# A two-block transformer kernel on one core: its weight stream fetched two units (1024 KB) at a time

## The chip, the core and the metric

The kernel runs on one core of a Trainium2 chip (trn2). The metric is the time of one execution on the device, in microseconds; of several runs the median counts. TensorE does the matrix products, VectorE, ScalarE and GpSimd the rest, and SyncE issues the transfers between HBM and SBUF, the memory on the core. In the profile the engines are called PE (PEld is its loading of weights), DVE, ACT, POOL and SP.

## The reference

A block on 256 rows of 2048 features, and a second block behind it. All is float32. Cut to what matters:

```python
def first_block(x, ...):
    h = rmsnorm(x, norm_mix_pre)
    proj = h @ w_in                                   # 2048 x 5120
    mix = concatenate([pool_mixer(...), hgrn2_mixer(...)]) @ w_out    # 2048 x 2048
    x = x + rmsnorm(mix, norm_mix_post)
    h = rmsnorm(x, norm_mlp_pre)
    ff = square(relu(h @ w_mlp_in)) @ w_mlp_out       # 2048 x 8192 x 2048
    return x + rmsnorm(ff, norm_mlp_post)

def second_block(x, c, ...):
    m = silu(c) @ ada_w + ada_b                       # six vectors of 2048: shifts, scales, gates
    n = modulate(rmsnorm(x), m[0], m[1])
    u, v = split(gelu(n @ a_w_in))                    # 2048 x 8192
    x = x + m[2] * ((u * spatial(rmsnorm(v))) @ a_w_out)
    n = modulate(rmsnorm(x), m[3], m[4])
    g, w = split(dwconv(n @ ffn_w_up))                # 2048 x 11264
    x = x + m[5] * ((silu(g) * w) @ ffn_w_down)       # 5632 x 2048
    return rmsnorm(x, final_g)
```

## The kernel before

**The weight stream.** All weights of the seven large products are cut on the host into 824 units (`wstream`, one unit is 128 partitions x 1024 float32, that is 256 rows of a weight matrix by 512 of its columns, 512 KB, 4 KB in a row per partition). The units are numbered in the order in which they are used. Eight units (six in the last four groups) make a group, a whole sum over 2048 inputs into 512 output columns, held in two PSUM banks (four in the up projection of the last stage). The groups: 0 to 9 input projection, 10 to 13 output projection of the mixers, 14 to 45 the MLP, 46 to 53 and 54 to 69 the gated stage, 70 to 103 the convolutional feed-forward.

**What happens to a unit.** Products are made in three passes at reduced format: each operand is a high part plus a low part. Unit n goes through slot n % 4 (`RING = 4`) of three rings in SBUF:

- SyncE (`unit(n)`, L290 to L294) waits until the low part of unit n-4 is made (the last reader of the slot in `raw`), and issues the transfer into `raw`.
- ScalarE (`split(n)`, L667 to L674) waits for the transfer and until TensorE has used unit n-4, and copies `raw` to the high part `whi`.
- VectorE (`split(n)`, L1064 to L1070) subtracts: `wlo = raw - whi`, and raises `lo_ready`.
- TensorE (`token_unit` L389, `feature_unit` L360, `wide_unit` L375) waits for `lo_ready` and multiplies; the last matmul of a unit raises `unit_used`.

Each engine runs its instructions in the order written. `body` (L676 and L1083) writes the splits of ScalarE and VectorE four units ahead of TensorE: while TensorE is at unit i of group j, they split unit i + 4. In between stand the work on the sums, the transposes' copies, and the norms.

**The other transfers.** SyncE issues everything from one list (L311 to L356). In groups 14 to 61 it also loads 192 pieces of `ada_w` (512 KB each, `ada(k)`, L296 to L300) into a ring of two, `aring`; VectorE adds each to `aacc` (L1080) behind the split that stands four units ahead. `ada_tile` (L62) puts them at units 1, 3, 5 and 7 of a group, in each eighth group at 0, 1, 2 and 3. Single rows of 2048 elements spread over 128 partitions (1024 KB, `row`, L302), `gvb` (L308, 256 KB) and pieces of `ws` (L305, 128 KB) stand at fixed units. A wait of SyncE holds back all that stands behind it.

**The start.** ScalarE squares the four parts of `x` as they come, splits unit 0 (L793), and only then takes the root of the norm (L794); VectorE, after that root, makes the normalised `xn`, which TensorE transposes first (L431).

**The places named below.** Before group 10 the heads are gated (`gate_heads`, L1260), squared, summed and scaled (`norm_heads`, L1274) and transposed (`heads_to_features`, L521), with splits of units 83 to 85 between these steps; L836 is the sigmoid of the gate's sums. In group 14 the root of the norm and the two functions of `relu2` (L873) stand between the splits of units 122 and 123. At the end of the MLP TensorE transposes `aacc` (`ada_columns`, L459) after the last piece was added. In group 46 `gelu_v` (L925) stands between the splits of units 378 and 379.

Of the kernel before, what the change touches and what calls it, by code (L numbers as in the profile page):

```python
# [19 lines left out]
RING = 4  # L20
# [41 lines left out]
def ada_tile(j, i):  # L62

    if not G_MLP <= j < G_MLP + VECS * 8:
        return None
    at = (0, 1, 2, 3) if (j - G_MLP) % 8 == 7 else (1, 3, 5, 7)
    return (j - G_MLP) * ADA_PER_GROUP + at.index(i) if i in at else None


def build(nc, xt, wstream, astream, cT, adab, gains, rows, gvrow, cwp, bsp, wsT, poolw, poolp, lbl, masks, corr,  # L70
          eye_in, out):
    ctx = ExitStack()
    with ctx:
# [4 lines left out]
        def region(size):  # L78
            o = at[0]
            at[0] += size  # L80
            assert at[0] <= base + SPAN, at[0] - base
            return o

        def place(name, offset, shape, dt=F32):
            return nc.alloc_sbuf_tensor_at(name, shape, dt, offset=offset)

        sem = lambda n: ctx.enter_context(nc.semaphore(n))
        KB = 1024

        raw = place("raw", region(16 * KB), [P, RING, UW])  # L90
# [91 lines left out]
        bank = [ctx.enter_context(nc.psum_tensor(f"bank{i}", [P, NC], F32)) for i in range(4)]  # L182
        mis = [ctx.enter_context(nc.psum_tensor(f"mis{i}", [P, NC], F32)) for i in range(4)]

        raw_arrived = [sem(f"raw_arrived{i}") for i in range(RING)]
        ada_arrived = [sem(f"ada_arrived{i}") for i in range(2)]
        x_arrived = [sem(f"x_arrived{i}") for i in range(4)]
        par_arrived = sem("par_arrived")
# [6 lines left out]
        lo_ready = sem("lo_ready")  # L195
# [92 lines left out]
        @block.sync  # L288
        def _(sp):
            def unit(n):  # L290
                if n >= RING:
                    sp.wait_ge(lo_ready, n - RING + 1)
                sp.dma_start(raw[:, n % RING, :], wstream[n:n + 1, :, :].rearrange("o p w -> p (o w)")
                             ).then_inc(raw_arrived[n % RING], 16)  # L294

            def ada(k):  # L296
                if k >= 2:
                    sp.wait_ge(ada_used, k - 1)
                sp.dma_start(aring[:, k % 2, :], astream[k:k + 1, :, :].rearrange("o p w -> p (o w)")
                             ).then_inc(ada_arrived[k % 2], 16)  # L300

            def row(r, dst):  # L302
                sp.dma_start(dst[:, :], rows[r:r + 1, :].to_broadcast([P, D])).then_inc(row_arrived[r], 16)

            def spatial_part(g):  # L305
                sp.dma_start(ws[:, 2 * g:2 * g + 2, :], wsT[:, 2 * g:2 * g + 2, :]).then_inc(ws_arrived, 16)

            def gv_part(g):  # L308
                sp.dma_start(gvb[:, :], gvrow[0:1, g * NC:(g + 1) * NC].to_broadcast([P, NC])).then_inc(gv_arrived, 16)

            for i in range(4):  # L311
                b, h = i % 2, i // 2
                sp.dma_start(x[:, b, h * 1024:(h + 1) * 1024], xt[:, b, h * 1024:(h + 1) * 1024]
                             ).then_inc(x_arrived[i], 16)
            for dst, src in ((gain, gains), (cf, cT), (eye, eye_in), (cw, cwp), (ab, adab), (bs, bsp)):
                sp.dma_start(dst[:], src).then_inc(par_arrived, 16)
            for n in range(RING):
                unit(n)
            for dst, src in ((pw, poolw), (pp, poolp), (lb2, lbl), (mk, masks), (cor, corr)):
                sp.dma_start(dst[:], src).then_inc(mix_arrived, 16)  # L320
            for n in range(RING, UNITS):
                unit(n)
                m = n - RING
                j, i = (m // GU, m % GU) if m < G_DT * GU else (G_DT, GU)
                if n == 78:
                    sp.wait_ge(h_sc, 18)
                    sp.wait_ge(p_d, 1)
                    row(ROW_MIX, gmix)
                if n == G_MLP * GU + RING:
                    sp.wait_ge(mix_lo, 8)  # L330
                    row(ROW_MLP, gmlp)
                    ada(0)
                    ada(1)
                if (k := ada_tile(j, i)) is not None and k >= 2:
                    ada(k)
                if n == (G_AV + 2) * GU:
                    sp.wait_ge(xs_lo, 24)
                    row(ROW_GATE, gate2)
                    gv_part(0)
                if G_AV < j <= G_AV + 4 and i % 4 == 2:  # L340
                    spatial_part(2 * (j - G_AV - 1) + i // 4)
                g = 4 * ((j - G_AU) // 8) + (j - G_AU) % 8
                if G_AU <= j < G_FF and (j - G_AU) % 8 < 4 and i == 3 and g < 7:
                    sp.wait_ge(vs_ready, g + 1)
                    gv_part(g + 1)
                if j == G_AU + 4 and i == 3:
                    row(ROW_GATE2, gate5)
                if j == G_AU + 12 and i == 3:
                    row(ROW_END, gend)
            sp.wait_ge(out_act, 1)  # L350
            sp.dma_start(out[:, 0, 0:3 * NC], acc[:, 0, 0:3 * NC]).then_inc(out_sent, 16)
            sp.wait_ge(out_dve, 1)
            sp.dma_start(out[:, :, 3 * NC:], acc[:, :, 3 * NC:]).then_inc(out_sent, 16)
            sp.wait_ge(out_dve, 2)
            sp.dma_start(out[:, 1, 0:3 * NC], acc[:, 1, 0:3 * NC]).then_inc(out_sent, 16)
            sp.wait_ge(out_sent, 48)  # L356
# [291 lines left out]
        def _(act):  # L648
# [18 lines left out]
            def split(n):  # L667
                if n >= UNITS:
                    return
                slot = n % RING  # L670
                act.wait_ge(raw_arrived[slot], 16 * (n // RING + 1))
                if n >= RING:
                    act.wait_ge(unit_used, n - RING + 1)
                act.activation(whi[:, slot, :], raw[:, slot, :], ACT.Copy).then_inc(hi_ready, 1)  # L674

            def body(j, evac, after=None, done=0, last=True):  # L676
                units = units_of(j)
                for i in range(units):
                    if i == units - 1 and evac:
                        evac()  # L680
                    if i >= done and (last or i < units - 1):
                        split(first_unit(j) + RING + i)
                    if after:
                        after(i)
# [28 lines left out]
            def features(z, j, first=None):  # L713

                feature_tmp(z, 0)
                for i in range(8):
                    if 0 < i < 7:
                        feature_tmp(z, i + 1)
                    act.wait_ge(tm_ready, 8 * z + i + 1)
                    act.activation(xs[:, 2 * i:2 * i + 2, 0:T], tiles(t1[:, i % 2, :]), ACT.Copy).then_inc(xs_hi, 1)  # L720
                    if i == 0:
                        feature_tmp(z, 1)
                    if first:
                        first(i)
                    if 2 <= i < 2 + RING:
                        split(first_unit(j) + RING + i - 2)
# [60 lines left out]
            for i in range(4):  # L787
# [3 lines left out]
                           ssq[:, S_X, b, h:h + 1])  # L791
            sums_read(S_X)
            split(0)  # L793
            root(S_X)  # L794
            split(1)
# [880 lines left out]
```

## Time and profile before

| | |
|---|---|
| median of 3 runs | 2459.76 us (2459.64 to 2462.09) |
| the profiled execution, its own time | 2461.96 us |
| its span in the profile | 2460.2 us |
| busy: TensorE, VectorE, ScalarE, GpSimd | 2396.0, 1663.1, 1191.2, 58.8 us |
| HBM read | 544.89 MB, 222 GB/s over the span |
| mean granted clock of TensorE | 0.990 |

The span goes from the first to the last instruction; the execution's own time is 1.8 us more. Busy times of different engines overlap. A row of a group of instructions (section 5 of the page) ends with the idle time of the engine just before them and what ended most of it; a time in square brackets in a timeline is the same for one instruction. The landing of a transfer is the time from its issue by SyncE to the last of its 16 completion signals. Times are counted from the first instruction.

### The profile page before, as it was taken

The numbers are of one execution on the slowest core, as the hardware profiler recorded it, in microseconds if no ns is written. First come the engines' busy times: TensorE is split into PE (matmuls) and PEld (weight loads), VectorE is DVE, ScalarE is ACT, GpSimd is POOL, SyncE is SP. The second block draws the span as 40 slices with busy tenths as digits, with TensorE's granted clock in tenths as the row PEclk, the third lists the DMA queues.
The fourth block names the chain that finished last, engine by engine and source line by source line (L and its number), as shares of the span: only waits on it lengthen the run. The fifth ranks groups of instructions, "written<-read, shape, count | busy, mean of one in ns | idle before, by whom it ended". The sixth has DMA issues, their size and how long they took to land.

```text
span 2460.2 us, 30688 instructions
## 1 busy us (share of the span) xinstructions
PE 2396.0 (97%) x12000; PEld 2032.0 (83%) x12000; DVE 1663.1 (68%) x1960; ACT 1191.2 (48%) x1508; POOL 58.8 (2%) x42
## 2 busy tenths in 40 slices
PE   7999999999999999997999999999999999999997
PEld 7989787888888888886888888887888888888886
DVE  5884666777677677677667776555767567765675
ACT  6553455544444534545554443445655355544553
POOL 0330000000000000000000000000000000000000
PEclk9999999999999999999999999999999999999999
DMA  6434555887887887875987886564555655565553
GB/s 226 137 129 163 170 188 179 307 286 273 284 288 272 277 294 279 272 273 189 351 291 264 276 297 223 186 198 153 188 188 188 195 184 188 187 194 191 184 177 137
DMA packets 152189, 549.00 MB, mean 223 GB/s; under 512 B 17776, under 2 KB 19056, under 8 KB 151280
## 3 DMA queue, kind: packets, MB, share of 16 engines
q1 hardware_dynamic: 152048, 547.05, 65.8%
q8 instruction: 97, 1.59, 0.3%
q14 instruction: 44, 0.36, 0.0%
HBM read 544.89 MB, written 2.10 MB: 222 GB/s over the span
## 4 chain that ended last, share of the span: by engine, by line
PE 93%; DVE 3%; ACT 2%; issue 1%; DMA 0%; SPq 0%; POOL 0%; DVEq 0%; ACTq 0%
PE bank L398 20%; PE bank L400 19%; PE bank L399 19%; PE bank L383 7%; PE mis L383 7%; PE bank L385 3%; PE mis L385 3%; PE bank L370 2%; PE bank L371 2%; PE bank L372 2%; PE mis L400 2%; PE mis L399 2%; PE mis L398 2%; PE mis L484 1%; PE mis L454 1%
## 5 line engine op out<-in xcount | busy, mean ns | idle before, releaser
L1069 DVE TENSOR_TENSOR wlo<-raw,whi 128x1024 fp32r<-128x1024 f32 x824 | 1005.2, 1225 | 688.4 <-ACT whi L674 685.9
L674 ACT ACTIVATE whi<-raw 128x1024 fp32r<-128x1024 f32 x824 | 868.1, 1059 | 1060.0 <-PE bank L400 660.4
L398 PE MATMUL bank<-whi,xs 128*128 128x512 f32 x1152 | 456.5, 396 | 4.3 <-DVE wlo L1069 2.8
L400 PE MATMUL bank<-wlo,xs 128*128 128x512 f32 x1152 | 450.1, 391 | 0.0
L399 PE MATMUL bank<-whi,xs 128*128 128x512 f32 x1152 | 450.0, 391 | 0.0
L398 PE MATMUL bank<-whi,hs 128*128 128x512 f32 x1072 | 419.5, 391 | 2.1 <-DVE hs L1549 2.1
L399 PE MATMUL bank<-whi,hs 128*128 128x512 f32 x1072 | 418.0, 390 | 0.0
L400 PE MATMUL bank<-wlo,hs 128*128 128x512 f32 x1072 | 417.9, 390 | 0.0
L398 PEld LDWEIGHTS bank<-whi,xs 128*128 128x128 f32 x1152 | 217.4, 189 | 50.1 <-issue 6.5
L400 PEld LDWEIGHTS bank<-wlo,xs 128*128 128x128 f32 x1152 | 217.1, 188 | 45.8
L399 PEld LDWEIGHTS bank<-whi,xs 128*128 128x128 f32 x1152 | 217.5, 189 | 44.0 <-issue 0.2
L383 PE MATMUL bank<-xs,whi 128*128 128x512 f32 x704 | 251.7, 402 | 0.8 <-issue 0.8
L383 PE MATMUL mis<-xs,whi 128*128 128x512 f32 x704 | 249.2, 399 | 0.0
L1080 DVE SCALAR_TENSOR_TENSOR aacc<-aring,sc_c,aacc 128x1024 f32<-128x1024 f32 x192 | 245.6, 1279 | 1.3 <-DMA aring<-astream 1.0
L398 PEld LDWEIGHTS bank<-whi,hs 128*128 128x128 f32 x1072 | 201.6, 188 | 44.1 <-DVE hs L1549 2.5
L400 PEld LDWEIGHTS bank<-wlo,hs 128*128 128x128 f32 x1072 | 201.7, 188 | 42.0
L399 PEld LDWEIGHTS bank<-whi,hs 128*128 128x128 f32 x1072 | 201.7, 188 | 41.8 <-issue 0.2
L385 PE MATMUL bank<-xs,wlo 128*128 128x256 f32 x704 | 198.7, 282 | 0.0
L385 PE MATMUL mis<-xs,wlo 128*128 128x256 f32 x704 | 197.9, 281 | 0.0
L383 PEld LDWEIGHTS bank<-xs,whi 128*128 128x128 f32 x704 | 133.3, 189 | 34.0 <-issue 1.2
L383 PEld LDWEIGHTS mis<-xs,whi 128*128 128x128 f32 x704 | 132.3, 188 | 32.8
L385 PEld LDWEIGHTS bank<-xs,wlo 128*128 128x128 f32 x704 | 134.1, 191 | 0.1
(180 smaller groups left out, 2118.6 us busy)
## 6 DMA issues: line engine op xcount, KB each, us to landing
raw<-wstream SPq DMA_DIRECT2D x824, 512.0 KB, 4.3
aring<-astream SPq DMA_DIRECT2D x192, 512.0 KB, 4.9
x<-xt SPq DMA_DIRECT2D x4, 512.0 KB, 6.4
gate<-rows SPq DMA_DIRECT2D x2, 1024.0 KB, 7.7
gvb<-gvrow SPq DMA_DIRECT2D x8, 256.0 KB, 5.2
out<-acc SPq DMA_DIRECT2D x2, 768.0 KB, 4.4
pw<-poolw SPq DMA_DIRECT2D x1, 1024.0 KB, 9.6
gmix<-rows SPq DMA_DIRECT2D x1, 1024.0 KB, 7.8
```

The lines of the kernel that those rows point to most:

```text
L370: pe.matmul(o, whi[:, slot, c], h, start=st, stop=False, skip_group_check=True)
L371: pe.matmul(o, whi[:, slot, c], l, start=False, stop=False, skip_group_check=True)
L372: mm = pe.matmul(o, wlo[:, slot, c], h, start=False, stop=sp_, skip_group_check=True)
L383: pe.matmul(banks[m][:, :], whi[:, slot, c], xs[:, kt0 + k, :], start=st, stop=False, skip_group_check=True)
L385: mm = pe.matmul(banks[m][:, 0:T], wlo[:, slot, c], xs[:, kt0 + k, 0:T], start=False, stop=sp_, skip_group_check=True)
L398: pe.matmul(o, h, whi[:, slot, c], start=first and k == 0, stop=False)
L399: pe.matmul(o, l, whi[:, slot, c], start=False, stop=False)
L400: mm = pe.matmul(o, h, wlo[:, slot, c], start=False, stop=last and k == UK - 1)
L454: mm = pe.transpose(mis[pair + m // 2][:, (m % 2) * T + b * P:(m % 2) * T + (b + 1) * P], t1[:, b, m * P:(m + 1) * P], eye[:, :])
L674: act.activation(whi[:, slot, :], raw[:, slot, :], ACT.Copy).then_inc(hi_ready, 1)
L1069: dve.tensor_tensor(wlo[:, slot, :], raw[:, slot, :], whi[:, slot, :].bitcast(F32), ALU.subtract).then_inc(lo_ready, 1)
L1080: dve.scalar_tensor_tensor(out=a, in0=aring[:, k % 2, :], scalar=sc_c[:, kt:kt + 1], in1=a, op0=ALU.mult, op1=ALU.add).then_inc(ada_used, 1)
```

## The change

The weights come in transfers of two units. `unit(n)` does nothing for an odd n; for an even n it issues one transfer for units n and n + 1 into slots n % 4 and n % 4 + 1. It waits until the low part of unit n-3 is made, since both slots must be free, and both units have one semaphore: ScalarE's split of either waits for the whole transfer. Source and destination have 128 partitions with two runs of 4 KB each.

```diff
-        raw_arrived = [sem(f"raw_arrived{i}") for i in range(RING)]
+        raw_arrived = [sem(f"raw_arrived{i}") for i in range(RING // 2)]
...
             def unit(n):
+
+                if n % 2:
+                    return
                 if n >= RING:
-                    sp.wait_ge(lo_ready, n - RING + 1)
-                sp.dma_start(raw[:, n % RING, :], wstream[n:n + 1, :, :].rearrange("o p w -> p (o w)")
-                             ).then_inc(raw_arrived[n % RING], 16)
+                    sp.wait_ge(lo_ready, n - RING + 2)
+                sp.dma_start(raw[:, n % RING:n % RING + 2, :], wstream[n:n + 2, :, :].rearrange("o p w -> p o w")
+                             ).then_inc(raw_arrived[n % RING // 2], 16)
...
                 slot = n % RING
-                act.wait_ge(raw_arrived[slot], 16 * (n // RING + 1))
+                act.wait_ge(raw_arrived[slot // 2], 16 * (n // RING + 1))
```

Lines behind the edit move down by three. The order of SyncE shows what stands where. At the start, before and with the change (`x` is the input, the small ones are parameters, `pw` and what follows belongs to the mixers):

```order
L313 DMA x<-xt 128x1024 x4
L316 DMA gain<-gains 128x64
...
L316 DMA ab<-adab 128x64
L316 DMA bs<-bsp 128x16
L293 DMA raw<-wstream 128x1024 x4
L320 DMA pw<-poolw 128x2048
```

```order
L316 DMA x<-xt 128x1024 x4
L319 DMA gain<-gains 128x64
...
L319 DMA ab<-adab 128x64
L319 DMA bs<-bsp 128x16
L296 DMA raw<-wstream 128x2x1024 x2
L323 DMA pw<-poolw 128x2048
```

Units 0 and 1 are one transfer now. In groups 46 to 48, units 382 to 388 of the stream, before:

```order
L293 DMA raw<-wstream 128x1024 x2
L299 DMA aring<-astream 128x1024
L293 DMA raw<-wstream 128x1024
L306 DMA ws<-wsT 128x256
L293 DMA raw<-wstream 128x1024
L299 DMA aring<-astream 128x1024
L293 DMA raw<-wstream 128x1024
L303 DMA gate_63<-rows 128x2048
L309 DMA gvb<-gvrow 128x512
L293 DMA raw<-wstream 128x1024
L299 DMA aring<-astream 128x1024
L293 DMA raw<-wstream 128x1024
```

The single `raw` ahead of `ws` is unit 382, the one behind it 383, the one ahead of `gate_63` 384, the one behind `gvb` 385, the last 386. With the change:

```order
L296 DMA raw<-wstream 128x2x1024
L302 DMA aring<-astream 128x1024
L296 DMA raw<-wstream 128x2x1024
L309 DMA ws<-wsT 128x256
L302 DMA aring<-astream 128x1024
L296 DMA raw<-wstream 128x2x1024
L306 DMA gate_63<-rows 128x2048
L312 DMA gvb<-gvrow 128x512
L302 DMA aring<-astream 128x1024
L296 DMA raw<-wstream 128x2x1024
```

The pair ahead of `ws` is 382 and 383, the one ahead of `gate_63` 384 and 385, the last 386 and 387. Each odd unit has moved up to the even one: unit 383 stands ahead of the piece of `ws`, unit 385 ahead of the row for `gate2` and of `gvb`. The pieces of `ada_w` stand behind the pair whose second unit they followed. On the other engines the order of instructions is the same.

## Rows read from the trace of the kernel before

**Rows 1.** The page: span, engines, and the costliest groups of the two splits.

```profile
span 2460.2 us, 30688 instructions
...
PE 2396.0 (97%) x12000; PEld 2032.0 (83%) x12000; DVE 1663.1 (68%) x1960; ACT 1191.2 (48%) x1508; POOL 58.8 (2%) x42
...
L1069 DVE TENSOR_TENSOR wlo<-raw,whi 128x1024 fp32r<-128x1024 f32 x824 | 1005.2, 1225 | 688.4 <-ACT whi L674 685.9
L674 ACT ACTIVATE whi<-raw 128x1024 fp32r<-128x1024 f32 x824 | 868.1, 1059 | 1060.0 <-PE bank L400 660.4
```

**Rows 2.** List of waits, whole span: who for whom, us in all, times, longest.

```profile
ACT whi L674 <- DMA raw<-wstream: 72.1, 39, 4.9
...
PE bank L398 <- DVE wlo L1069: 2.8, 3, 1.7
...
PE bank L398 <- DVE hs L1549: 2.1, 1, 2.1
```

**Rows 3.** Tile view of raw: time from issue to landing over 824 transfers.

```profile
DMA to landing us min/median/max: 3.0/4.3/9.9
```

**Rows 4.** Timeline of the start (first and last row); tile view, transfer issued at 6.85.

```profile
12.08 1.06 ACT L674 ACTIVATE whi<-raw 128x1024 fp32r<-128x1024 f32 x1 [1.01 <-DMA raw<-wstream]
...
DMA to landing us min/median/max: 6.5/6.5/6.5
...
15.26 1.09 PE L431 MATMUL mis<-eye,xn 128*128 128x128 f32 x4 [15.26 <-DVE xn L1125]
```

**Rows 5.** Timeline around unit 82: SyncE, VectorE, ScalarE, TensorE.

```profile
297.40 0.33 SPq L293 DMA_DIRECT2D raw<-wstream  x1
...
298.73 4.62 DVE L1069 TENSOR_TENSOR wlo<-raw,whi 128x1024 fp32r<-128x1024 f32 x4
...
300.76 1.06 ACT L674 ACTIVATE whi<-raw 128x1024 fp32r<-128x1024 f32 x1 [1.61 <-DMA raw<-wstream]
304.22 1.28 ACT L836 ACT_TABLE_LOAD   x1 [2.40 <-PE bank L400]
...
318.95 0.33 PE L526 MATMUL mis<-eye,oo 128*128 128x128 f32 x1 [1.22 <-DVE oo L1274]
```

**Rows 6.** Timeline around unit 122: ScalarE, VectorE, TensorE.

```profile
428.30 1.06 ACT L674 ACTIVATE whi<-raw 128x1024 fp32r<-128x1024 f32 x1 [0.24 <-DMA raw<-wstream]
...
434.08 1.23 DVE L1069 TENSOR_TENSOR wlo<-raw,whi 128x1024 fp32r<-128x1024 f32 x1 [3.39 <-ACT whi L674]
...
436.72 0.48 PE L398 MATMUL bank<-whi,xs 128*128 128x512 f32 x1
```

**Rows 7.** Timeline of TensorE at the end of the MLP.

```profile
1117.50 1.75 PE L461 MATMUL mis<-eye,aacc 128*128 128x128 f32 x14 [0.86 <-DVE aacc L1080]
```

**Rows 8.** Timeline around unit 378 by engine; DMA view (KB, us to landing) from 1161.3.

```profile
1160.84 0.91 SPq L293 DMA_DIRECT2D raw<-wstream  x2
...
raw<-wstream SPq DMA_DIRECT2D x1, 512.0 KB, 5.6
...
1164.97 1.06 ACT L674 ACTIVATE whi<-raw 128x1024 fp32r<-128x1024 f32 x1 [4.63 <-DMA raw<-wstream]
...
1170.92 1.23 DVE L1069 TENSOR_TENSOR wlo<-raw,whi 128x1024 fp32r<-128x1024 f32 x1 [3.63 <-ACT whi L674]
...
1172.55 0.39 PE L398 MATMUL bank<-whi,xs 128*128 128x512 f32 x1
```

**Rows 9.** Timeline around unit 387: SyncE, ScalarE, VectorE, TensorE.

```profile
1179.10 0.33 SPq L293 DMA_DIRECT2D raw<-wstream  x1
...
1187.37 1.06 ACT L674 ACTIVATE whi<-raw 128x1024 fp32r<-128x1024 f32 x1 [1.51 <-DMA raw<-wstream]
...
1191.89 1.23 DVE L1069 TENSOR_TENSOR wlo<-raw,whi 128x1024 fp32r<-128x1024 f32 x1 [2.21 <-ACT whi L674]
...
1194.31 0.39 PE L398 MATMUL bank<-whi,xs 128*128 128x512 f32 x1
```

**Rows 10.** Windows view: us, busy by engine, PEclk, DMA share, GB/s.

```profile
2392.00:2396.00 4.00, 4.00 (x12) 3.13 (x11) 0.64 (x2) 0.60 (x1) 0.00 (x0) 0.57 0.66 218
```

## The prediction

> **What bounds the kernel now.** I read the page first. TensorE is busy 2396.0 of 2460.2 us [rows 1], so the kernel is matmul bound, and a change of the weight transfers can only act through the 64 us in which TensorE stands still. The next question is how far the weight stream is from making it stand. The rows of the two split instructions say: ScalarE (L674, 1059 ns) waits mostly for a free slot, that is for TensorE (660.4 us), VectorE (L1069, 1225 ns) waits for ScalarE [rows 1]. In the list of waits ScalarE waits for a weight transfer 39 times, 72.1 us in all, but TensorE waits for VectorE's low part only 3 times, 2.8 us in all [rows 2]. So late weights are common and almost always hidden. Hidden by what, and by how much, decides the case.
>
> **The two covers in the steady state.** A unit of 12 matmuls takes TensorE 2.72 us: unit 379 starts at 1172.55 and unit 387 at 1194.31, eight units in 21.76 us [rows 8, 9]. ScalarE starts to split unit n when TensorE ends unit n-4; call that time t. The low part is done at t + 1.06 + 1.23 = t + 2.3, TensorE wants it at t + 3 x 2.72 = t + 8.2: the second cover is 5.9 us. The transfer of unit n leaves when the low part of unit n-4 is done, at t + 2.3 - 10.9 = t - 8.6, and lands 4.3 us later in the median [rows 3]: the first cover is 8.6 - 4.3 = 4.3 us.
> With the change the pair (n, n+1) leaves when the low part of unit n-3 is done, at t - 5.9, since its second slot must be free too. It carries 1024 KB. What that costs: at the start the transfers run back to back, and units 0 and 1 land at 12.06 and 6.85 + 6.5 = 13.34 [rows 4], so 512 KB more are 1.28 us more. The pair should land after 4.3 + 1.3 = 5.6 us, 0.3 us before it is wanted. No row shows a 1024 KB weight transfer; its bounds are the shortest landing, 3.0, plus 1.3 = 4.3 us and twice the median, 8.6 us. I take 5.6, since both pieces are rows of 4 KB as before and the extra bytes have a measured price. The loop of one pair of slots (landing 5.6, two splits 2.1, the last low part 1.2) is 8.9 us, and TensorE needs 10.9 us for its four units. So the steady stretches, nearly all of the kernel, gain and lose nothing: the first cover is spent, the second still stands. The Trainium skill, "DMA: Bandwidth & Descriptors", section "Measured", gives 6.15 us of data movement for 1 MB; the trace moves 512 KB in 1.28 us at the start, so it does not agree, and by the page's figure alone the pair would land over 3 us later than I take, past its first cover and still inside the second.
>
> **Where a cover is missing.** I went through all places where TensorE starts less than 3 us after the low part, or waits. Six of them hang on a transfer. Each is priced in the time frame of before.
> 1. **Start.** TensorE's first work waits for VectorE, at 15.26. Behind it stands a chain: ScalarE splits unit 0 at 12.08, when its transfer lands, and only then takes the root for the norm [rows 4]. The pair lands with unit 1, at 13.34: **+1.3**.
> 2. **Heads before the output projection.** Unit 82 left at 297.40 and ScalarE waited for it until 300.76. VectorE ends the low part of unit 79 at 298.73 + 1.2 = 299.9; the pair (82, 83) leaves then and lands after at least 3.3 + 1.3 us, at 304.6, that is 3.8 later. ScalarE stood idle 2.40 us before 304.22, which absorbs 2.4; the other 1.4 us go down the chain of gates and norms to the transposes at 318.95, for which TensorE already waits 1.22 us [rows 5]: **+1.4**.
> 3. **First MLP group.** ScalarE waits for unit 122 until 428.30; its pair lands 1.3 us later by the price of the bytes, or up to twice that if unit 123 queues as it does now, and the chain after the split (root, two relus, split of 123) follows without a gap that would absorb it. The low part of unit 123 is done at 434.08 + 1.23 = 435.31 and wanted at 436.72 [rows 6], cover 1.4: between 0 and +1.1, I take **+0.6**.
> 4. **End of the MLP.** TensorE waits 0.86 us for the last modulation step of VectorE [rows 7], which stands in its order behind the low parts of units 366 and 367. Unit 366 lands up to 1.3 later as the first half of a pair; what VectorE idles between them takes some of it: between 0 and 1.3, **+0.7**.
> 5. **First gated group.** Unit 378 lands at 1164.95, unit 379, issued at 1161.3, after 5.6 us, at 1166.9: the pair is 2.0 later. ScalarE works without a gap from there to the split of 379; its low part ends at 1170.92 + 1.23 = 1172.15, wanted at 1172.55 [rows 8]. Cover 0.4: **+1.6**.
> 6. **The burst behind it.** Here a 1024 KB row, a 256 KB row and modulation weights share the queue. Unit 387 left at 1179.10 and needed the longest landing of all, 9.9 us [rows 3, 9]; unit 386 was split at 1187.37. The pair lands not before 1189.0, +1.6, and up to 2 us later still, because the pair (382, 383) is late by about 2 and the low part of 383 releases this pair. Cover at unit 387: 1194.31 - 1191.89 - 1.23 = 1.2. Between +0.4 and +2.4, I take **+1.6**.
> Sum: 1.3 + 1.4 + 0.6 + 0.7 + 1.6 + 1.6 = **+7.2 us**. Against the gains: SyncE issues 412 transfers less, but it waits for slots nearly all the time, so that is worth nothing. Unit 385 now stands ahead of the 1024 KB row instead of behind it, but TensorE did not wait for it, so this gains nothing either.
> The modulation transfers keep their places behind the odd units; they are asked for four splits ahead of their use, and where two follow each other (last group of eight) SyncE waits for the ring of two anyway.
>
> The profiled execution took 2461.96 us (span 2460.2); its forecast is 2469.2. The median of the three runs is 2459.76, 2.2 us less, and from there the sum gives **2467.0 us**, slower by 0.3%. About 0.2%, 4.9 us, is what can be told from no change.
>
> **Rivals.**
> A. *Not slower: the landing hardly grows.* Some 1.7 us of each landing do not depend on the bytes (3.0 shortest, less 1.28 for the data), and they are paid once per pair. If the crowded landings (4.3 and above, up to 9.9) contain such waits, a pair lands with or before its old second unit. Then places 3, 4 and 6 cost nothing and 5 under 1, while 1 and part of 2 stay, since they come from bytes and from the later issue: +2 to +4, about 2463. For it: the shortest and the median landing differ by 1.3 us at the same size. Against it: three of the six prices are simply "the pair is there when its second half was there". Chance 0.29. It decides if pairs land within about 4.5 us in quiet stretches.
> B. *The ring becomes the bound in the crowded stretches.* From group 14 to 61 the modulation weights share the queue. If pairs land there after 8.0 us and more, the loop is 8.0 + 2.1 + 1.2 = 11.3 against 10.9 us, 0.4 us for each four of 384 units, 38 us if it holds everywhere, 13 us if in a third of them, on top of the 7. Against it: a queue that works through the same bytes does not land the second half later than now. Result 2480 (at worst 2505). Chance 0.12. The Trainium skill, "Perfetto Trace Analysis", section "DMA Optimizations", says that splitting transfers may let work start sooner; the change does the opposite, and places 1 and 2 are where the trace agrees, with units 0 and 82 awaited as they land (12.06, 300.74).
> C. *The clock.* After TensorE's idle gap of 2.1 us (the wait for the product's low part) it ran at a mean of 0.57 of its clock for 4 us, so mostly at 1.2 instead of 2.4 GHz [rows 2, 10]. 4 x 0.43 = 1.7 us is the price. Place 2 makes the gap before 318.95 1.2 + 1.4 = 2.6 us, so the clock may fall there: +1.7, 2468.7. This is inside the forecast's range.
> D. *Faster.* The only waits for weights that could go are 2.8 and 0.86 us, and the start costs 1.3: at best -2.4 us, which is no change. Beyond 0.2% only if a stretch at half clock vanishes as well. Chance 0.04.
> That the change does not do what it says is excluded by the order of SyncE: 412 issues of two units, no other engine moved.
>
> **The numbers.** Forecast with its own range of +5 to +12: 0.55; B 0.12: slower 0.67. A within 0.2%: 0.29. Faster 0.04. The range leaves out no more than 2 in 10: below, it takes in most of A (+1.7, 2461.5); above, it takes in the upper bounds of places 3, 4 and 6 (+0.5, +0.6, +0.8) and of 2 and 5 if a quiet pair lands 2 us later (+2 each), and C (+1.7), and leaves out most of B: +16, 2476.
>
> **What would show it.** Right: landings of 1024 KB near 5.6 us; ScalarE waiting for transfers far more often than 39 times and over 200 us in all, with TensorE's total wait for low parts up from 2.8 by only a few us; first matmul at 16.5; the gap before L526's transposes 2.6 us; TensorE standing short of low parts near 1172 and 1194. Wrong: quiet pairs landing near 4.3 us (A), or small waits of TensorE spread over every group from 14 to 61 (B), or the first matmul still at 15.3.

## The result, and the profile after

The changed kernel takes **2471.89 us** (median of 7 runs, 2468.57 to 2475.63); the kernel before, run beside it, 2460.14 (7 runs, 2459.64 to 2465.67). The ratio is 1.0041 with a 95% interval of 1.0028 to 1.0054: slower by 10 us, between 7 and 13 (the two medians by themselves lie 11.8 us apart). Forecast were 2467.0, a range of 2461.5 to 2476.0, and slower with 0.67.

The profiled execution took 2468.57 us, the shortest of the seven, against a forecast of 2469.2 for it and 2461.96 before: +6.6 us. That is what this profile can explain; the rest of the 10 us stands further below.

The page after the change, span, engines, the two splits and the weight transfer (columns as in [rows 1]; the last row is transfers, KB each, median us to landing):

```profile
span 2466.8 us, 30276 instructions
PE 2396.5 (97%) x12000; PEld 2030.3 (82%) x12000; DVE 1660.8 (67%) x1960; ACT 1187.7 (48%) x1508; POOL 58.8 (2%) x42
L1072 DVE TENSOR_TENSOR wlo<-raw,whi 128x1024 fp32r<-128x1024 f32 x824 | 1002.8, 1224 | 704.9 <-ACT whi L677 704.0
L677 ACT ACTIVATE whi<-raw 128x1024 fp32r<-128x1024 f32 x824 | 864.9, 1058 | 1089.2 <-PE bank L403 430.4
...
raw<-wstream SPq DMA_DIRECT2D x412, 1024.0 KB, 4.9
```

Its list of waits, and the landing in the tile view of `raw`:

```profile
ACT whi L677 <- PE bank L403: 430.4, 283, 9.3
ACT whi L677 <- DMA raw<-wstream: 351.2, 129, 6.3
...
PE bank L401 <- DVE wlo L1072: 5.4, 6, 1.7
```

```profile
DMA to landing us min/median/max: 4.7/4.9/9.0
```

TensorE's busy time is the same, 2396.5 against 2396.0 us [rows 1]. Its **idle time, span less busy, grew from 64.2 to 70.3 us, +6.1**. ScalarE's waits for transfers grew from 72.1 us in 39 [rows 2] to 351.2 us in 129, and took the place of waits for a slot (660.4 us [rows 1], now 430.4): the first cover is gone. TensorE's waits for low parts grew only from 2.8 to 5.4 us: the second one stands. So the idle time must lie in a few places, and the timeline has them. Rows of TensorE after the change (start, duration; the idle time before it in square brackets):

```profile
16.50 1.73 PE L434 MATMUL mis<-eye,xn 128*128 128x128 f32 x7 [16.50 <-DVE xn L1128]
...
320.72 1.54 PE L529 MATMUL mis<-eye,oo 128*128 128x128 f32 x6 [2.88 <-DVE oo L1277]
...
439.33 0.47 PE L401 MATMUL bank<-whi,xs 128*128 128x512 f32 x1
...
1120.63 1.64 PE L464 MATMUL mis<-eye,aacc 128*128 128x128 f32 x13 [1.25 <-DVE aacc L1083]
...
1139.75 0.66 PE L434 MATMUL mis<-eye,xn 128*128 128x128 f32 x2 [11.68 <-DVE xn L1128]
...
1177.31 0.47 PE L401 MATMUL bank<-whi,xs 128*128 128x512 f32 x1 [1.24 <-DVE wlo L1072]
...
1197.87 0.47 PE L401 MATMUL bank<-whi,xs 128*128 128x512 f32 x1 [0.84 <-DVE wlo L1072]
1201.30 0.47 PE L401 MATMUL bank<-whi,xs 128*128 128x512 f32 x1 [0.47 <-DVE wlo L1072]
```

Before, the first stood at 15.26 [rows 4], the second waited 1.22 [rows 5], the row at 1120.63 waited 0.86 [rows 7], the transposes at 1139.75 waited 11.46, and the last three did not wait. The differences: 1.24 + 1.66 + 0.39 + 0.22 + 1.24 + 0.84 + 0.47 = 6.06 us, all of the 6.1 that the page shows. Behind each stands a pair that came late. ScalarE's rows for three of them:

```profile
304.91 1.06 ACT L677 ACTIVATE whi<-raw 128x1024 fp32r<-128x1024 f32 x1 [4.27 <-DMA raw<-wstream]
305.99 1.28 ACT L839 ACT_TABLE_LOAD   x1
...
1169.99 1.06 ACT L677 ACTIVATE whi<-raw 128x1024 fp32r<-128x1024 f32 x1 [6.31 <-DMA raw<-wstream]
...
1195.40 1.06 ACT L677 ACTIVATE whi<-raw 128x1024 fp32r<-128x1024 f32 x1 [5.91 <-DMA raw<-wstream]
```

Unit 82 stood there at 300.76 [rows 5] and the sigmoid's table load at 304.22; both are later, and the 2.40 us that ScalarE stood idle between them are used up: the load follows at once. At 1169.99 it is unit 378 (before 1164.97 [rows 8]), at 1195.40 unit 386 (its pair was issued at 1186.88, so it landed after 8.5 us).

### The profile page after: what moved, and what is told of

Its sections match the earlier page's. It is cut to its first block, busy times and chain, and to the rows that moved or that the text cites. A ratio compares the mean times of both kernels' runs of the same rounds, so it can differ in the third digit from the quotient of the medians.

```text
span 2466.8 us, 30276 instructions
## 1 busy us (share of the span) xinstructions
PE 2396.5 (97%) x12000; PEld 2030.3 (82%) x12000; DVE 1660.8 (67%) x1960; ACT 1187.7 (48%) x1508; POOL 58.8 (2%) x42
## 4 chain that ended last, share of the span: by engine, by line
PE 90%; DVE 4%; ACT 2%; DMA 2%; issue 1%; SPq 0%; POOL 0%; DVEq 0%; ACTq 0%
PE bank L401 19%; PE bank L403 19%; PE bank L402 19%; PE bank L386 7%; PE mis L386 7%; PE bank L388 3%; PE mis L388 3%; PE bank L373 2%; PE bank L374 2%; PE bank L375 2%; PE mis L403 2%; PE mis L401 2%; PE mis L402 2%; DMA raw<-wstream 2%; DVE wlo L1072 1%
## 5 line engine op out<-in xcount | busy, mean ns | idle before, releaser
L677 ACT ACTIVATE whi<-raw 128x1024 fp32r<-128x1024 f32 x824 | 864.9, 1058 | 1089.2 <-PE bank L403 430.4
```

## The experiments

Twelve kernels, timed in three groups, each beside the kernel before: median 2461.23 of 16 runs for e1 to e4, 2461.36 of 33 for e5 to e8, 2461.87 of 27 for e9 to e12. The last column is TensorE's idle time in the one profile of each kernel (span less busy) against the 64.2 us of before; it leaves the clock out, since work at half clock counts as busy. What a wait has grown by is taken against the wait before the same matmul in the kernel before.

| kernel | median us (runs) | ratio, 95% | idle against before |
|---|---|---|---|
| the change | 2471.89 (7) | 1.0041 (1.0028, 1.0054) | +6.1 |
| e9, the change again | 2472.19 (5) | 1.0042 (1.0030, 1.0055) | +7.9 |
| e1, late issue only | 2461.49 (11) | 1.0002 (0.9993, 1.0010) | +1.1 |
| e2, joint wait only | 2475.28 (5) | 1.0061 (1.0048, 1.0074) | +12.4 |
| e3, pair 82 undone | 2468.77 (6) | 1.0033 (1.0021, 1.0045) | +6.2 |
| e4, pair 0 undone | 2471.41 (5) | 1.0045 (1.0032, 1.0058) | +5.7 |
| e5, 15 pairs undone | 2464.42 (11) | 1.0010 (1.0002, 1.0019) | +0.5 |
| e10, only pair 82 | 2465.95 (11) | 1.0014 (1.0005, 1.0023) | +1.5 |
| e11, only 13 pairs from 366 | 2466.49 (11) | 1.0016 (1.0008, 1.0025) | +4.8 |
| e6, pairs, `raw` of six | 2467.16 (11) | 1.0022 (1.0013, 1.0031) | +3.5 |
| e7, before, root first | 2459.86 (11) | 0.9992 (0.9983, 1.0001) | -1.6 |
| e8, e6 with root first | 2464.16 (11) | 1.0010 (1.0001, 1.0019) | +0.9 |
| e12, before, root first, `raw` of five | 2459.10 (11) | 0.9991 (0.9982, 1.0000) | -2.2 |

### The two halves of the change: late issue (e1) and joint wait (e2)

e1 keeps single transfers with a semaphore each, but the even unit is released only when the pair would be:

```diff
-                    sp.wait_ge(lo_ready, n - RING + 1)
+                    sp.wait_ge(lo_ready, n - RING + 2 - n % 2)
```

> One half of the change alone: transfers of one unit with their own semaphores, but the even unit is issued only when the low part of unit n-3 is made, together with the odd one. Theory (late release and joint landing both count, and the pair is late mostly because it waits for its second half): start at 15.3, the gap before the transposes at 319 at 1.2 to 1.6, gated group +0.5 at most: +0.5 to +1.5 us in all. Rival (the late release is what costs): +5 to +7, with places 2 and 6 as in the changed kernel.

e2 issues as before, but both units of a pair have one semaphore, so the split of either waits for both:

```diff
-                             ).then_inc(raw_arrived[n % RING], 16)
+                             ).then_inc(raw_arrived[n % RING // 2], 16)
...
-                act.wait_ge(raw_arrived[slot], 16 * (n // RING + 1))
+                act.wait_ge(raw_arrived[slot // 2], 32 * (n // RING + 1))
```

> The other half alone: transfers of one unit issued as before, but both units of a pair share a semaphore, so that the split of the even unit waits until both have landed. Theory: start +1.3, unit 82 waits for unit 83 (landing 303.5 instead of 300.7, less 2.4 us of idle: +0.4), first MLP group 0 to +1.1, end of MLP about +1, gated groups +3: in all +5 to +8 us, nearly the whole change. Rival (late release costs): under +3.

The late issue by itself can't be told from no change. It is not quite free: the mean granted clock that is listed with each run is 0.9915 over e1's runs and 0.9906 over those of before, and at the same listed clock e1 is 1.5 us longer (at 0.991 a mean of 2462.9 us in four runs against 2461.3 in six, at 0.992 2460.9 in five against 2459.4 in two). Its profile shows where: ScalarE waits for transfers 134.7 us in 72 instead of 72.1 in 39, TensorE's gap before the heads' transposes is 1.39 instead of 1.22 us, and one new wait of 0.81 us stands near 1190:

```profile
320.30 1.09 PE L526 MATMUL mis<-eye,oo 128*128 128x128 f32 x8 [1.39 <-DVE oo L1274]
...
1190.77 0.47 PE L398 MATMUL bank<-whi,xs 128*128 128x512 f32 x1 [0.81 <-DVE wlo L1069]
```

The joint wait costs more than the whole change, +14 us. The largest of its new waits of TensorE:

```profile
581.31 0.87 PE L461 MATMUL mis<-eye,aacc 128*128 128x128 f32 x6 [2.00 <-DVE aacc L1080]
...
762.56 1.97 PE L461 MATMUL mis<-eye,aacc 128*128 128x128 f32 x16 [1.60 <-DVE aacc L1080]
...
1126.37 3.63 PE L461 MATMUL mis<-eye,aacc 128*128 128x128 f32 x16 [3.13 <-DVE aacc L1080]
...
1184.80 0.47 PE L398 MATMUL bank<-whi,xs 128*128 128x512 f32 x1 [1.57 <-DVE wlo L1069]
```

The sum over `aacc` is late where TensorE transposes it. With e2's order a piece of `ada_w` stands between the even and the odd unit: SyncE issues a single at 1105.49 and the next only at 1113.03, behind a piece that waited for its slot until 1112.65. The even unit then waits for a transfer that is not yet issued. In the changed kernel the odd unit has moved ahead of that piece, and in its first profile the waits at 581 and 762 are gone (e3 has 0.70 us there at 579.74, and the second profile of the change 0.55 at 940.27). So in the crowded stretches what costs is that an even unit waits for the odd one. That e2 costs more than the change fits the moved order and the one transfer, but no run has the order of the change with two transfers and one semaphore, so the two are not told apart.

At unit 82 the halves do not add up. Either alone is hidden, and only both together cost. ScalarE's split of unit 82, e1 and e2:

```profile
304.49 1.06 ACT L674 ACTIVATE whi<-raw 128x1024 fp32r<-128x1024 f32 x1 [4.08 <-DMA raw<-wstream]
...
304.08 1.06 ACT L674 ACTIVATE whi<-raw 128x1024 fp32r<-128x1024 f32 x1 [4.05 <-DMA raw<-wstream]
```

Counted from the end of unit 79's low part (299.95 before, 301.12 in e1, 300.82 in e2, 300.08 with the change), the split stands at 0.8 us before, 3.4 in e1, 3.3 in e2 and 4.8 with the change. The delays are 2.6, 2.5 and 4.0 us; ScalarE's 2.40 us of idle time take the first two up to 0.2 and 0.1, which is what TensorE's gap grows by (1.39 and 1.31 against 1.22), and leave 1.6 of the third.

### Which pairs cost: undone one by one (e3, e4, e5), done alone (e10, e11)

These five have both forms of `unit(n)`; units for which `alone(n)` holds come as single transfers, as before. `arrival` counts the landings of each semaphore.

```diff
+        def alone(n):
+            return n in (82, 83)
+        def arrival(n):
+            own = n if alone(n) else n - n % 2
+            return own % RING, sum(1 for m in range(own % RING, own + 1, RING) if alone(m) or m % 2 == 0)
...
-                act.wait_ge(raw_arrived[slot // 2], 16 * (n // RING + 1))
+                act.wait_ge(raw_arrived[arrival(n)[0]], 16 * arrival(n)[1])
```

e3 is `n in (82, 83)`, e4 `n < 2`, e5 `n < 2 or n in (82, 83) or 366 <= n < 392`, e10 `n not in (82, 83)`, e11 `not 366 <= n < 392`.

> The changed kernel, with units 82 and 83 alone in transfers of their own, issued as before. Theory: the gap before the transposes near 319 goes back from 2.88 to 1.2 to 1.4 us, and the half clock behind it (from 320.0, 6.8 us) goes with it, so 1.5 us of waiting and up to 3.4 us of half clock are saved against the changed kernel: 3 to 5 us in the profile. Rival (the clock falls at 320 by chance, not by the gap): only 1.5 us are saved and a half clock stretch is still there in the profile.

> The changed kernel, with units 0 and 1 in transfers of their own. Theory: TensorE's first work is at 15.3 again instead of 16.5, all else is unchanged: 1.2 us less than the changed kernel. Rival (the start is bound by something else, the root or the norm): the first work stays at 16.5.

> The changed kernel, with transfers of one unit only where the sum put a price: units 0 and 1, 82 and 83, 366 to 391 (15 transfers of the 412 are undone), pairs everywhere else. Theory: first work at 15.1, gap before the transposes 1.2 us, no wait near 1172, 1191, 1194: within 1.5 us of the kernel before, although 397 transfers stay paired. Rival (small losses are spread over the crowded groups): still 4 us or more slower than before.

> The kernel before with one single pair, units 82 and 83. Theory: one pair of 412 gives the gap of 2.9 us before the transposes (1.6 us more) and a stretch at half clock behind it (1.7 to 3.1 us): +3 to +5 us. Rival (the gap alone): +1.6.

> The kernel before with pairs only for units 366 to 391 (13 pairs). Theory: places 4, 5 and 6 and the norm chain at the end of the MLP: +4 to +6 us. Rival (they need the shift and crowding of the paired stream before them): under +3.

**e5 and the steady stretches.** 397 of 412 pairs are in place, and ScalarE waits as in the changed kernel, while TensorE's waits for low parts are nearly those of before (2.8 us in 3):

```profile
ACT whi L689 <- DMA raw<-wstream: 332.6, 131, 5.9
...
PE bank L413 <- DVE wlo L1084: 3.0, 4, 1.7
```

Idle time grew by 0.5 us: 0.25 before unit 123 at 436.17, which is place 3, and 0.32 before the transposes of `aacc` at 578.14. The median is 3 us above before all the same (0.5 to 4.7 by the interval); the mean of the listed clocks is 0.9897 here against 0.9902 over the runs of before beside it, which makes 1.2 us of 2462. All else, 15 pairs of 412 cause: the ratio falls from 10 us above before to 2.5.

**e10, e3 and unit 82.** One pair of 412, done alone, makes the kernel 4 us longer (1 to 6 by the interval), more than the wait that it adds:

```profile
320.60 1.97 PE L541 MATMUL mis<-eye,oo 128*128 128x128 f32 x8 [3.02 <-DVE oo L1289]
```

3.02 - 1.22 = 1.8 us of wait. What else happens there the windows show (PEclk, the granted clock as a share of the full one, is the third number from the end). Before the change:

```profile
320.00:324.00 4.00, 4.00 (x19) 3.27 (x18) 2.30 (x3) 1.07 (x2) 0.00 (x0) 1.00 0.69 210
324.00:328.00 4.00, 4.00 (x19) 3.31 (x18) 3.95 (x6) 2.50 (x5) 0.00 (x0) 1.00 0.87 311
```

With the change:

```profile
320.00:324.00 4.00, 3.28 (x12) 2.99 (x13) 2.94 (x4) 0.05 (x1) 0.00 (x0) 0.50 0.85 265
324.00:328.00 4.00, 4.00 (x13) 3.10 (x13) 1.23 (x1) 1.53 (x2) 0.00 (x0) 0.64 0.70 259
```

In e10 (from 324 to 328 its share is 1.00 again):

```profile
320.00:324.00 4.00, 3.40 (x13) 3.07 (x14) 3.94 (x4) 0.87 (x1) 0.00 (x0) 0.57 0.74 226
```

After the longer gap TensorE runs at 1.2 instead of 2.4 GHz. In the changed kernel it works 3.28 us at 0.50 and 4.00 us at 0.64, which loses 3.28 x 0.50 + 4.00 x 0.36 = 3.1 us; in e10 3.40 x 0.43 = 1.5. e4 (gap 2.89) and e9 (2.93) show the same fall. With e3 the gap is 1.22 us again and the clock stays full, from 324 to 328 as well:

```profile
320.00:324.00 4.00, 4.00 (x22) 3.47 (x23) 2.22 (x2) 0.69 (x1) 0.00 (x0) 1.00 0.83 270
```

e3's median is 2 to 3 us below the changed kernel's; the intervals of the two overlap, so this only agrees with e10. Its idle time did not fall below that of the change (+6.2): the 1.66 us at place 2 are gone, but others came in this one profile. The transposes of `aacc` at 579.74 wait 0.70 us, TensorE waits 0.31 us for a low part at 1233.08, and the transposes behind the norm at the end of the MLP, at 1136.39 before, waited 11.46 us there and wait 12.31 here (11.68 in the changed kernel). The last was not in my list.

**e4, the start, and the seventh place.** TensorE's first work is at 15.11 again, so the pair 0 is the cause of +1.24. The times do not show it: the ratio is 1.0045, that of the change 1.0041. The mean listed clock of e4's five runs, 0.9884, is the lowest of all kernels, which may hide it. In its profile the same transposes behind the norm stand out:

```profile
1126.30 1.06 ACT L689 ACTIVATE whi<-raw 128x1024 fp32r<-128x1024 f32 x1 [3.62 <-DMA raw<-wstream]
...
1139.95 2.79 PE L446 MATMUL mis<-eye,xn 128*128 128x128 f32 x12 [12.69 <-DVE xn L1140]
```

The row of 1126.30 is unit 370. Before it was split at 1122.31, when TensorE had freed the slot; now its pair lands after that, and the sums of the norm stand behind it on ScalarE and VectorE. This costs 0.22 us in the changed kernel's profile, 1.0 in e11's and 1.2 in those of e4 and e9: it hangs on how late that one landing is.

**e11, the end of the MLP and the gated stage.** 13 pairs make 4.8 us of idle time. TensorE's rows:

```profile
1117.86 1.97 PE L476 MATMUL mis<-eye,aacc 128*128 128x128 f32 x16 [1.52 <-DVE aacc L1095]
1137.77 2.79 PE L446 MATMUL mis<-eye,xn 128*128 128x128 f32 x12 [12.47 <-DVE xn L1140]
...
1177.67 0.47 PE L413 MATMUL bank<-whi,xs 128*128 128x512 f32 x1 [1.35 <-DVE wlo L1084]
...
1198.82 0.47 PE L413 MATMUL bank<-whi,xs 128*128 128x512 f32 x1 [1.64 <-DVE wlo L1084]
```

They wait 0.66 us more before `aacc` (place 4), 1.01 for the norm (7 in the list below), 1.35 at place 5 and 1.64 at place 6: 0.66 + 1.01 + 1.35 + 1.64, and 0.46 more before unit 387 at 1202.25, 5.1 us in all; its first work stands 0.3 us earlier than before, which leaves the 4.8. With e10's 1.8 and the start's 1.2 that is 7.8, between the 6.1 of the changed kernel's first profile and the 7.9 of its second. In time, by the ratios, e10 is 3.4 and e11 3.9 us above before; with 1.2 for the start that is 8.5 of the 10.

### The change once more (e9)

No edit.

> The changed kernel itself, beside the next three on one chip. Waits account for 7.0 us (span without the half clock time: 2451.4 against 2444.4); the median is 10 to 12 above before. Theory (the rest is the half clock behind the longer gap at 318 to 321): +9 to +12, and the stretch at half clock is there again. Rival (the rest is chance): +6 to +8.

The median is the same within 0.3 us. TensorE's largest gaps are the same ones, with other amounts: 2.93 at 320.65, 1.37 at 1121.31, 12.70 at 1141.47, 1.20 at 1180.86, 1.31 at 1201.72 and 0.42 at 1205.15; the first work stands at 16.29. One is new: 0.55 before the transposes of `aacc` at 940.27.

### A deeper ring (e6), and the start taken off the transfer (e7, e8, e12)

e6 gives `raw` six slots, three pairs; a pair is then issued two units earlier.

```diff
+RAW = 6
-        raw = place("raw", region(16 * KB), [P, RING, UW])
+        raw = place("raw", region(24 * KB), [P, RAW, UW])
...
-                    sp.wait_ge(lo_ready, n - RING + 2)
+                    sp.wait_ge(lo_ready, n - RAW + 2)
```

> The changed kernel with six slots in the ring of raw instead of four (24 KB instead of 16), so that a pair can leave one pair earlier; bytes, joint landing and order of SyncE are as in the changed kernel. Theory (a pair is late only where it leaves late or behind a queue): only the start keeps its 1.2 us, places 2 to 6 shrink to a third or less: +1 to +3 us against before. Rival (the joint landing alone costs, as the separate run of it suggests): +7 or more stays.

I had expected 1 to 3 us; it is 5.8 in the median and 3.5 in idle time; what makes the other 2 us is open. ScalarE's waits for transfers fell to 95.4 us in 29, and place 2 is back at 1.22 us with the full clock. Left are the start (first work at 16.40) and the places where the queue is crowded:

```profile
1120.06 1.97 PE L465 MATMUL mis<-eye,aacc 128*128 128x128 f32 x16 [1.67 <-DVE aacc L1084]
...
1178.78 0.47 PE L402 MATMUL bank<-whi,xs 128*128 128x512 f32 x1 [1.12 <-DVE wlo L1073]
```

Issuing earlier helped at unit 82, where the queue is quiet; in the crowded places waits are left, as if the even unit still waited there for the bytes of both (its longest landing is 12.5 us). That reason is argued, not shown.

e7 is the kernel before with ScalarE and VectorE's norm ahead of unit 0 instead of behind its split; e8 is the same edit on e6, e12 on the kernel before with `raw` of five slots.

```diff
-            split(0)
             root(S_X)
+            split(0)
...
             variance(S_X, 2)
-            split(0)
...
-            features(0, lambda i: normalised(0, S_X, i), 0, first=lambda i: split(1 + i) if i < 3 else None)
+            features(0, lambda i: normalised(0, S_X, i), 0, first=lambda i: [split(m) for m in ((0, 1) if i == 0 else (1 + i,))] if i < 3 else None)
```

> The kernel before, but ScalarE takes the root of the first norm ahead of the split of unit 0, and VectorE makes xn ahead of its low part. Theory: the weight transfer is off the path of the first work; the root waits for the variance at 11.3 only, and TensorE's first work moves from 15.3 to about 12.7; the first product, which needs unit 0 and the features, moves from 18.7 to 16.5 to 17: -1 to -2 us. Rival (features or the clock bound the start): within 0.5 us of before.

> Pairs with six slots of raw and the root of the first norm ahead of the splits. Theory: the last cost of the pairs, the start, is gone as well: -1.5 to +1 us against before. Rival: the start keeps +1.2 because the first product needs the pair anyway, +1 to +3.

> Transfers of one unit, five slots of raw instead of four, root of the first norm ahead of the split of unit 0. Theory: the start gives 1 to 2 us as in the run of it alone, the fifth slot takes the 2.8 and 0.9 us of waits near 1117 and 1172 to 1194 at best: -2 to -4 us against before. Rival (those waits are not for transfers): -1.5 as with the root alone.

In e7 the first work stands at 12.69 instead of 15.26 and the first product at 16.51 instead of 18.73:

```profile
12.69 2.79 PE L431 MATMUL mis<-eye,xn 128*128 128x128 f32 x12 [12.69 <-DVE xn L1125]
...
16.51 0.39 PE L370 MATMUL bank<-xs,whi 128*128 128x256 f32 x1 [1.03 <-DVE xs L1139]
```

So the wait of TensorE's first work for a weight transfer was a matter of order. With pairs this is so for the first work (12.53 in e8), but not for the first product: it stands at 17.32, 0.8 us later than in e7, since ScalarE splits units 0 and 1 only at 13.15, when the pair has landed, and the transposes' copies stand behind them. That is the rival that I had named, and e8's time, +3 us, lies where it put it and not where the theory did. With e5 it is the best form with pairs. e12 has the lowest median, 2.8 us under before, with an interval that ends at no difference; its fifth slot left the waits at the heads (1.22 us) and at `aacc` (0.90) where they were, so a further slot does not help there, and the forecast, whose range the median meets, was wrong on what that slot does. All that can be said of it is that it is not slower than before, and faster than every kernel with pairs.

## Why the prediction was right

The mechanism is the one forecast: the steady stretches hide the pairs, and a few chains with a split in them do not. The size was low: +7.2 us forecast, 10 measured (11.8 between the medians, 4.9 above the 2467.0), inside a range that was wide enough for it. (The upper bounds from which the range was made add up to +14.8; the +16 has 1.2 us more that no term names.) That the profile's own time, 2468.57, is so near its forecast of 2469.2 is in part luck, as the account of the clock below shows.

**The covers.** The quiet pair lands after 4.9 us, not 5.6. The step that was too high took the median single, 4.3, and added 1.28 for the bytes; but the median single holds more than the shortest one, 3.0 [rows 3], and this more is not paid again. Pair against single it is 4.7 against 3.0 at the shortest, 4.9 against 4.3 in the median, 9.0 against 9.9 at the longest (10.1 in e9). The conclusion, that steady stretches gain and lose nothing, held with more room than I gave it: e5.

**The places.** Predicted, and found in the rows (first profile; second, e9, where it differs by over 0.3; e1 to e11 where they say more):
1. Start +1.3: 1.24. e4 and e7 show the cause.
2. Heads +1.4: 1.66; the pair left at 300.11 and landed in 4.8 us where I took 4.6. e3 and e10 show the cause, e1 and e2 that it takes the late issue and the joint landing together.
3. First MLP group +0.6: nothing. TensorE reached unit 123 at 439.33, and its low part was done 0.14 us earlier: of the cover of 1.4 us all but that was used. In e4 and e5, which have this pair too, TensorE waits 0.21 and 0.25 us.
4. End of the MLP +0.7: 0.39, and 1.52 - 0.86 = 0.66 in e11.
5. Gated group +1.6: 1.24.
6. Burst behind it +1.6: 0.84 + 0.47 = 1.31 (e9: 1.73). The larger wait is at unit 386, for which I had computed no cover, the smaller at 387. The pair (386, 387) landed after 8.5 us, where unit 387 alone had needed 9.9 [rows 3].
7. Not in the list: the norm's sums behind unit 370, +0.22 (e9: +1.24). I had gone through the places where TensorE has under 3 us of cover over a *low part*. Here TensorE waits for a norm, and a split stands in that norm's chain. The places 1 and 2 were of the same sort, so the search should have gone through all chains in which a split stands, not through those two alone.

The sum was 7.2 and the rows give 6.1 and, in the second profile, 7.9. In the first profile places 3 to 6 were priced 1.6 us too high together, and places 2 and 7 cost 0.5 more than the list had.

**Rival C** was put at 1.7 us "may fall there", outside the sum. This is the step that was mis-sized. The clock fell in all four profiles with the gap of 2.9 to 3.0 us, and lost 1.5 (e10) to 3.1 us there. It belonged in the sum. Why TensorE's busy time is the same in the first profile all the same: it got time back elsewhere. Near 396, behind a wait of 4.36 us for the norm, before the change:

```profile
396.00:400.00 4.00, 2.09 (x10) 2.12 (x11) 3.82 (x6) 2.00 (x5) 1.58 (x1) 0.50 0.58 236
400.00:404.00 4.00, 3.34 (x10) 2.45 (x9) 2.17 (x4) 2.62 (x6) 0.00 (x0) 0.50 0.44 135
404.00:408.00 4.00, 4.00 (x17) 3.21 (x16) 0.76 (x2) 1.11 (x3) 0.00 (x0) 0.77 0.00 0
```

With the change (the same work is 4.6 us later):

```profile
402.00:403.00 1.00, 0.45 (x2) 0.48 (x3) 1.00 (x3) 0.00 (x0) 0.22 (x1) 0.50 1.00 414
403.00:404.00 1.00, 1.00 (x6) 1.00 (x6) 1.00 (x3) 0.33 (x1) 0.00 (x0) 0.50 1.05 430
404.00:405.00 1.00, 1.00 (x7) 0.94 (x5) 0.86 (x1) 0.97 (x3) 0.00 (x0) 0.50 0.38 152
405.00:406.00 1.00, 0.34 (x3) 0.03 (x1) 0.69 (x1) 0.91 (x4) 0.00 (x0) 0.82 0.09 33
```

The loss was 2.09 x 0.50 + 3.34 x 0.50 + 4.00 x 0.23 = 3.6 us and is 2.45 x 0.50, plus up to 0.34 x 0.50, = 1.4: 2.2 us are back. A like stretch behind a wait for a norm, near 1700 before and 1706 after, costs 3.5 us before and 3.0 after by the same count: another 0.5. The third place is the start. Two matmuls of the same kind that follow each other, before and with the change:

```profile
22.95 0.41 PE L371 MATMUL bank<-xs,whi 128*128 128x256 f32 x1
23.16 0.41 PE L372 MATMUL bank<-xs,wlo 128*128 128x256 f32 x1
...
20.18 0.28 PE L374 MATMUL bank<-xs,whi 128*128 128x256 f32 x1
20.30 0.28 PE L375 MATMUL bank<-xs,wlo 128*128 128x256 f32 x1
```

They follow at 0.21 us before and at 0.12 with the change. Before, the slow pace lasts from the first product at 18.73 until 23.4; with the change it is gone from 20.2 on, and from 20 to 24 us TensorE does 34 matmuls instead of 22. That is about 2.0 us gained, and the share listed for these windows, 1.00 in both, does not show it. It is no merit of the pairs: the pace is the fast one from the first or second product on in the change, e9, e4 and e7, and slow until somewhere between 20 and 25 us in the ten others, e2, e3 and e6 with a late start among them. Against all this, TensorE lost 4.00 x 0.42 = 1.7 us near 88, below. Together 3.1 + 1.7 - 2.2 - 0.5 - 2.0 = 0.1 us: even, and by luck. The stretches elsewhere (2.2, 0.5 and 2.0 back, 1.7 lost) made this profile 3.0 us shorter than the waits and the clock at 320 alone would have.

Over all runs it does not even out. The mean granted clock of the changed kernel's runs is 0.9896 and 0.9898 (7 and 5 runs), that of before 0.9903 in the last group; 0.0005 to 0.0007 of 2466 us are 1.2 to 1.7 us. Compared at the same listed clock, 0.990, the four runs of the change have a mean of 2469.7 us and those of before 2461.4 to 2462.2 in the three groups, +7.5 to +8.3; e9's runs lie 7.7 to 9.6 above before at equal clock. Waits of 6 to 8 us and a clock of 1 to 2 make up most of the 10. The listed clock has steps of 0.001, 2.5 us, so this split is no finer than that. It also leaves out the slow pace of the start, which the listed clock does not show. How the 10 us divide on average stays open.

**Rival A** had the mechanism half right: the fixed part is paid once per pair, and landings hardly grew. Quiet pairs land at 4.7 to 4.9, close to the 4.5 from which it was to decide. It failed in its second half: a pair that lands when its second half used to is late for its first half, and e2 shows that this costs. **B** did not happen: TensorE's waits for low parts are six, 5.4 us, and e5 has four, 3.0 us, against three of 2.8 before. **D** did not either.

**What was to be seen:** first work at 16.5 (16.50), the gap at L526's transposes of 2.6 (2.88), ScalarE over 200 us (351.2) in far more than 39 waits (129), TensorE short near 1172 and 1194 (gaps before 1177.31 and 1201.30, the same work 5 and 7 us later): right. Landings near 5.6: wrong, 4.9.

## What to carry to other kernels

When transfers are joined, ask for each consumer of a first half what chain hangs on it: in the steady state a ring's second cover absorbed 397 joint transfers for half a microsecond of TensorE's time, and 15 others, at the start and where a norm, a gate or a sum is waited for, cost nearly all. Count a longer gap of TensorE with the clock that follows it, and look for such chains on the engine that does the waiting, not only where TensorE waits for the tile itself. Joining had nothing to give here: SyncE stood waiting for low parts 1806 of 2460 us before the change, 777 times, so its issues were not the bound. If joining must be, leave single units at the corners, or keep chains from standing behind a transfer (root first).

## What the runs showed of the hardware

**Joint landing.** 512 KB more in one transfer cost 1.7 us at the shortest (3.0 to 4.7) and 0.6 in the median, against the 1.28 us between the landings of units 0 and 1 at the start of the kernel before. The Trainium skill, "DMA: Bandwidth & Descriptors", section "Measured", gives 6.15 us of movement alone for 1 MB, measured on transfers issued from GpSimd; the trace does not agree for these, issued by SyncE, since here the whole way from issue to landing took 4.7 to 4.9 us.

**The clock behind a gap.** At one and the same place TensorE kept 2.4 GHz behind gaps of 1.22 us (before, e3, e5, e6, e7, e8, e11, e12), 1.31 (e2) and 1.39 us (e1), and fell to 1.2 GHz behind 2.88, 2.89, 2.93 and 3.02 us (the change, e4, e9, e10). A pair's wait of 1.7 us thus cost 1.5 to 3.1 us more.

**Elsewhere the clock differs from run to run.** Behind the gap of 1.92 us near 88 it was full before and 0.58 over four microseconds after the change, with 1.93 us of gap. The gap is 1.92 to 1.94 in all fourteen profiles, and the clock fell behind it in four of them (the change, e9, e1, e6), so here the length of the gap alone does not decide:

```profile
88.00:92.00 4.00, 4.00 (x23) 4.00 (x22) 4.00 (x4) 1.34 (x2) 3.37 (x3) 0.58 0.56 159
```

Such stretches, and the slow pace at the start (0.21 us from one 128x256 matmul to the next instead of 0.12, until 23.4 us before and gone from 20.2 after the change, with 1.00 listed in both), make runs of one kernel differ by several microseconds, and a single profile can't settle differences of this size.
